# Moving one of the eight batches of compressed cache pages from the last round of the first projection to the second half of the first gate projection

## What is computed

```python
def compress(rows, w):      # rows (B,L,KV,HD), w (CMP_LEN,KV); CMP_LEN 32, CMP_STRIDE 16
    n = L // CMP_STRIDE
    seg = rows[:, :n * CMP_STRIDE].reshape(B, n, CMP_STRIDE, C_KV_HEADS, HEAD_DIM)
    first = jnp.einsum('bnrhd,rh->bnhd', seg, w[:CMP_STRIDE])
    second = jnp.einsum('bnrhd,rh->bnhd', seg, w[CMP_STRIDE:])
    return first[:, :-1] + second[:, 1:]
...
    h = h + mix
    h = h + jax.nn.sigmoid(h @ prm['w_ple_gate'][i]) * (p[i] @ prm['w_ple'][i])
```

## Time and profile before

| | |
|---|---|
| median of 3 runs | 2066.35 us (2063.69 to 2068.67) |
| span of the profiled execution | 2066.1 us |
| PE busy | 1915.6 us, 93% |
| DVE busy | 1063.6 us, 51% |
| ACT busy | 833.9 us, 40% |
| chain that ended last | PE 77%, DVE 11%, SP's queue 4%, DMA 3% |
| line 1541 in that chain | 44% of the span |

### The profile page before, as it was taken

The page is one execution under the profiler, slowest core; times in us unless marked ns, Lnnn a source line. Parts: engine busy times, 40 slices in busy tenths (PEclk is TensorE's granted clock), DMA queues, the critical chain, the costliest instruction groups (busy, mean ns, idle before and its releaser), DMA issues.

```text
span 2066.1 us, 43255 instructions
## 1 busy us (share of the span) xinstructions
PE 1915.6 (93%) x16603; PEld 1621.0 (78%) x16603; DVE 1063.6 (51%) x1777; ACT 833.9 (40%) x1761; POOL 1.4 (0%) x8
## 2 busy tenths in 40 slices
PE   4999999999999899998999997899999777879998
PEld 3899999888888799798999995444444467769998
DVE  3358777666443544346689665433333322235454
ACT  2344444554344333445755552333323322234454
POOL 0000000000000000000000000000000000000000
PEclk9999999999999799999999999999999899999999
DMA  5788878633877488576555552244444389885454
GB/s 192 232 269 263 263 257 265 206 113 123 267 263 247 146 280 272 203 233 202 157 151 162 162 155 75 92 139 132 136 130 136 116 286 295 286 280 188 170 179 139
DMA packets 306536, 406.05 MB, mean 197 GB/s; under 512 B 18472, under 2 KB 222823, under 8 KB 305088
## 3 DMA queue, kind: packets, MB, share of 16 engines
q1 hardware_dynamic: 306384, 403.94, 61.3%
HBM read 391.43 MB, written 12.45 MB: 195 GB/s over the span
## 4 chain that ended last, share of the span: by engine, by line
PE 77%; DVE 11%; SPq 4%; DMA 3%; issue 2%; ACT 2%; DVEq 0%; ACTq 0%
PE PJ L1541 44%; PE XB L1993 8%; PE XB L1567 4%; PE XB L2004 4%; DVE w_low L980 2%; SPq L490 2%; DVE scr L999 2%; SPq L496 1%; PE XB L1813 1%; PE PJ L1981 1%; PE XB L1656 1%; DMA cring<-in_cache_c_win_kv_dram 1%; PE PJ L1960 1%; PE XB L1585 1%; PE XB L2063 1%
## 5 line engine op out<-in xcount | busy, mean ns | idle before, releaser
L1541 PE MATMUL PJ<-xh,w_up 128*128 128x264 f32 x3072 | 920.2, 300 | 40.1 <-DVE w_low L980 21.5
L1541 PE MATMUL PJ<-xl,w_up 128*128 128x264 f32 x3072 | 881.0, 287 | 0.0
L1541 PE MATMUL PJ<-xh,w_low 128*128 128x264 f32 x3072 | 879.3, 286 | 0.0
L980 DVE TENSOR_TENSOR w_low<-wring,w_up 128x512 fp32r<-128x512 f32 x768 | 524.8, 691 | 606.0 <-ACT w_up L602 595.6
L602 ACT CAST w_up<-wring 128x512 fp32r<-128x512 f32 x768 | 473.3, 619 | 644.7 <-PE PJ L1541 536.9
L1541 PEld LDWEIGHTS PJ<-xh,w_up 128*128 128x128 f32 x3072 | 587.6, 191 | 79.8 <-issue 56.4
L1541 PEld LDWEIGHTS PJ<-xl,w_up 128*128 128x128 f32 x3072 | 587.7, 191 | 1.4
L1541 PEld LDWEIGHTS PJ<-xh,w_low 128*128 128x128 f32 x3072 | 585.6, 191 | 0.0
L1993 PE MATMUL XB<-wring,proj 128*32 128x512 f32 x320 | 167.1, 605 | 1.1 <-DVE proj L1419 0.9
L2004 PEld LDWEIGHTS XB<-const,cring 128*128 128x128 f32 x640 | 70.8, 141 | 86.1 <-ACT wring L926 41.9
L1412 DVE COPY wring<-XB 128x512 f32<-128x512 f32 x80 | 55.3, 691 | 159.6 <-PE XB L2004 159.6
(11 more groups left out here) (301 smaller groups left out, 1448.7 us busy)
## 6 DMA issues: line engine op xcount, KB each, us to landing
wring<-in_w_in_ab_dram SPq DMA_DIRECT2D x144, 512.0 KB, 4.6
cring<-in_cache_c_cmp_kv_dram SPq DMA_DIRECT2D x128, 512.0 KB, 3.9
cring<-in_cache_c_sel_kv_dram SPq DMA_DIRECT2D x256, 256.0 KB, 2.9
wring<-in_w_in_c_dram SPq DMA_DIRECT2D x112, 512.0 KB, 3.7
wring<-in_w_ple_gate_dram SPq DMA_DIRECT2D x64, 512.0 KB, 3.6
cring<-in_cache_a_kv_dram SPq DMA_DIRECT2D x48, 512.0 KB, 5.0
wring<-in_w_out_ab_dram SPq DMA_DIRECT2D x32, 512.0 KB, 5.2
cring<-in_cache_c_win_kv_dram SPq DMA_DIRECT2D x64, 256.0 KB, 4.1
```

The source lines that it names most:

```text
L980: nc.vector.tensor_tensor(w_low[:, e % NE], raw(e), w_up[:, e % NE].bitcast(F32), ALU.subtract).then_inc(sem("w_lo"), 1)
L1541: ins = nc.tensor.matmul(PJ[(2 * bl + c) % 4][:, 0:T], w[:, e % NE, k, tileT(c)], x[:, kx, :], start=(kx == 0 and w is w_up and x is xh), ...
```

## The change

Batch 4 no longer goes with AB1's fifth round. AB1's first four rounds take batches 0 to 3, OUT0 takes 4 and 5 (before 5 and 6), and GATE0 takes 6 in its first four blocks (before 7) and 7 in its last four, which had no pages. The counts of `c_used`, `c_in` and `cmp_free` follow. DVE copies batch 6 out before block 4's splits instead of before block 5's, and batch 7 after the whole gate. SP's loop of AB1 runs four times and the fifth round's quarters are written out.

```diff
-        CMP_A, AK, AV, CMP_B = 0, 80, 104, 128
+        CMP_A, AK, AV, CMP_B = 0, 64, 88, 112
@@ SP
             for m in range(8):
                 for q in range(4):
                     quarter(GATE0 + m, w_g, 0, m, q)
-                    if m < 4:
-                        page(2, 5, m, q)
+                    page(2 + m // 4, 4, m % 4, q)
...
-            sp.wait_ge(sem("c_used"), NP + CMP_B + 48)
+            sp.wait_ge(sem("c_used"), NP + CMP_B + 64)
             sp.dma_start(wg, w_c[:, :, 40 * P:40 * P + 48]).then_inc(sem("wg_in"), 16)
@@ DVE
-                if n % 4 == 3:
+                if n % 4 == 3 and n < 16:
                     compressed(n // 4, n // 4, CMP_A)
...
                 for m in range(8):
-                    if layer == 0 and m == 5:
-                        compressed(2, 7, CMP_B)
+                    if layer == 0 and m == 4:
+                        compressed(2, 6, CMP_B)
...
+                if layer == 0:
+                    compressed(3, 7, CMP_B)
@@ PE
-            ab1_round(4, True)
+            ab1_round(4, True, False)
...
             def beside_gate(m, s):
-                if m < 4:
-                    beside_out(8 + m, s)
+                beside_out(8 + m, s)
```

## The result

| | before | after |
|---|---|---|
| median | 2066.05 us (4 runs, 2063.69 to 2068.67) | 2085.19 us (4 runs, 2082.50 to 2087.97) |
| ratio | | 1.0091, 95% interval 1.0073 to 1.0109 |
| span of the profiled execution | 2066.1 us | 2080.2 us (its time: 2082.59) |

The changed kernel is slower by 19.1 us, 0.9%. The forecast was +3.6 us, and its range ended at +6.7. The two profiled spans differ by less, 14.1 us: after's profiled execution was one of its quicker ones, and before's probably its slowest.

What follows compares the result with a forecast made beforehand. PE was taken to bound the kernel at both places, its chain lying on PE for 77% of the span. Terms of -13.15 + 14.28 + 2.5 = +3.6 us on a 2066.35 median gave 2070 us, range 2066.5 to 2073.0.

Steps and rivals of the forecast that it cites:

- Term 1: AB1's last round without its 16 pages: 12.8 us a block, paced by DVE's split, 51.2 for 64.35 us, -13.15 us.
- rival at PE's pace: AB1's last round: DVE's splits just make it, blocks take 12.53 us; sum +2.5 us, 2068.8; chance 0.13.
- Term 2: Gate blocks 4 to 7 with the pages added: PE-bound, no hidden room, +14.28 us.
- rival of cheaper pages: Gate blocks 4 to 7: pages cost some 6.2 us and not 14.28; 2061.9 in all; chance 0.05.
- Term 3: End of the gate: PE's embedding transposes wait for DVE's two copies of batch 7, nothing hides it, +2.5 us.
- SP's new wait and the spill: SP's queue behind the last page: `wg` issued later, spill landing near 982.5 against 988.0; cost nothing, cover 5 us.
- cold start: CQ's first matmuls at half clock for longer, or a late spill: +6.9 us, 2073.3; chance 0.17.
- SP loses 16 pages from its queue: AB1's last round: DMA engines 0.79 busy and PE not waiting for them, so SP's shorter queue is worth nothing.
- The last section of the prediction: Signs expected in the profile of after; forecast wrong if AB2, OUT0 or layer 1 change length.

Runs made afterwards that it cites:

- e12: Changed kernel with SP's value loop written out, four reciprocals of the norm in AB1's last round left out; 2068.24 us in one run.
- e4: Changed kernel without the join: embedding transposed into banks the pages don't use, so PE doesn't wait for DVE's copies; 2078.49 us, ratio 1.0065.
- e2: Changed kernel with SP's code shifted by 32 more unused semaphore increments, 144 in all by the trace's count; 2071.79 us, ratio 1.0035.
- e1: Kernel before with SP's code shifted by 96 unused semaphore increments, no work moved; 2073.56 us, ratio 1.0037.
- e3: Kernel before with SP's code shifted by 128 unused semaphore increments; 2066.06 us, ratio 1.0002.
- e5: Kernel before with SP's code shifted by 32 unused semaphore increments; 2065.33 us, ratio 0.9994.
- e6: Kernel before with SP's code shifted by 64 unused semaphore increments; 2064.73 us, ratio 0.9994.
- e9: Kernel before with SP's value loop written out as straight code; 2064.15 us, ratio 0.9985.
- e13: Kernel before with SP's code shifted by 224 unused semaphore increments; 2071.39 us in one run.
- e15: Kernel before with SP's code shifted by 112 unused semaphore increments; 2074.75 us in one run.
- e8: Changed kernel with SP's value loop written out as straight code, unshifted; 2067.65 us, ratio 1.0011.
- e7: Changed kernel with SP's code shifted by 32 more and the embedding's transposes freed of the wait for DVE's copies; 2069.98 us, ratio 1.0014.
- e10: Changed kernel with SP's value loop written out and the embedding's transposes freed of the wait for DVE's copies; 2066.76 us, ratio 0.9993.
- e11: Changed kernel with batch 7 neither loaded nor multiplied, its place filled from batch 6's sums, leaving only AB1's lighter round; 2055.71 us, ratio 0.9947.

## Why the prediction was wrong

**Term 1, the round at 51.2 us: right.** 51.31 us, blocks at 12.84, DVE's split ahead of slot 7 as said, and e12 shows the bound itself. The rival at PE's pace is out.

**Term 2, the pages in the gate: right.** Blocks of 15.78, 16.21 and 16.22 us against 15.8, 16.2 and 16.2. The rival of cheaper pages is out.

**Term 3, the join: right in kind, 0.9 us too dear.** 2.5 us were forecast, at least 2.0, and 1.6 measured (e4 against after); PE stands idle for 1.45 us, not 2.3. The step missed is that the last page itself now stands ahead of PE's last sum. DVE's last operation on `hs` starts 1.29 us behind the last matmul of the projection in both kernels (970.57 - 969.28, and 971.67 - 970.38), but PE comes to its last sum 0.82 us behind that matmul in place of 0.12, so 0.7 us of DVE's copies lie beside the page. That the path up to CQ's steady pace came out at +3.56 against +3.6 is luck: 1.4 us more between the spatial mix and the embedding's product made up for it, of which the forecast had nothing.

**SP's new wait and the spill: right.** `wg` was issued 9.5 us later, and ACT lost nothing by it. The spill landed 10.5 us after its issue in place of 7.4, at 984.2, 4.9 us ahead of ACT's first split. The cold start cost nothing that shows: from the transposes to CQ's steady pace it took 17.78 us, and 17.73 before.

**The step that failed** is the one that gave SP's part nothing, in two sentences: "SP loses 16 pages from its queue ...; nothing" and "I would be wrong if AB2, OUT0 or layer 1 change their length, since nothing there is touched". Each instruction that SP gained was priced by its own time in the queue, hidden. None was priced by its place in the code. The change adds 112 instructions to an engine whose loop lies behind them; in the bad stretch that costs two gaps of some 8 us at a point where ACT and PE live from SP's transfers, and 13.4 us of time by the medians (after against e2; 11.6 by the ratios). The last section of the prediction did name the symptom, layer 1 changing its length, but without a mechanism or a chance. It needed one: the rows on the packets and SP's timeline at the jump were in the trace of before. They couldn't have told where the bad stretch lies; they could have made it a rival on the slower side. The Trainium skill's page "Runtime: NRT & Kernel Launch", section "Instruction fetch mechanics", says that a taken branch whose target isn't in the window of code at hand forces a DMA fetch before execution goes on. The trace agrees in kind: 5.84 us of "issue" at the jump, and 15 packets for 6. The page's blocks are of 16 KiB; here the packets of this queue have 8 KB, and the shifts fit a period of 8 KB.

**A second, smaller miss is the profile's place among the runs.** The prediction took the span, 2066.1, for the profiled execution's time. In each later run the time is 2 us or so over the span (2082.59 against 2080.2), so the profiled execution of before took about 2068 and was probably the slowest of its three runs, 2068.67, not 0.25 us under the median. Five other traces with before's layer 0 (e1, e3, e5, e6, e9) reach the embedding's transposes at 965.4 to 968.0, mean 967.0 (e13 to e15 give 966.5), not at 969.85; after, e2 and e8 at 972.8 on the mean. So the cost of the change up to there is +5.8 us, not +3.5. By parts, mean of those three minus mean of those five:

| stretch, by first starts | difference |
|---|---|
| to the transposes behind AB1 (L1610) | -13.3 |
| from there to the spatial mix (L1750) | +0.4 |
| from the mix to the embedding's product (L1817) | +1.8 |
| from there to the gate's first sum (L1524), all of it in the product | +1.0 |
| from the gate's first sum to its last | +14.3 (forecast 14.3) |
| from the last sum to the embedding's transposes (L1837) | +1.6 (forecast 2.5) |

The +1.0 comes from the clock and not from the change: the product takes 17.0 and 17.1 us at a mean granted clock of 0.83 and 0.82 in before and after, and 15.5 us at 0.91 in e5 and e8. Most of the +1.8 sits in the mix, whose matmuls are the same in number. Busy by stretch from its first to just past its last start, before and after; the granted clock is the third number from the end:

```profile
685.63:706.29 20.66, 20.66 (x77) 15.15 (x75) 4.14 (x9) 1.40 (x3) 0.00 (x0) 0.64 0.29 96
```

```profile
671.73:693.61 21.88, 21.88 (x76) 15.96 (x74) 4.13 (x9) 1.40 (x3) 0.00 (x0) 0.59 0.27 88
```

PE is busy throughout in both, and the clock falls to 1.2 GHz within them; after, it falls sooner relative to the work (mean 0.59 for 0.64). By the rows of L1750 the mix takes 19.7 to 20.1 us in the nine traces with before's layer 0, 21.2 to 21.4 in after, e2, e4, e7, e8 and e10, but 19.4 in e11, which has done the same work up to there, and 16.9 in e12. What shifts the fall stays open, and so whether the change brings it; it isn't the gate's pages, which come later. Together: -13.3 + 2.2 + 1.0 + 14.3 + 1.6 = +5.8 us, where e2 measured +5.7 on the medians and +7.2 by its ratio. With e8 the cost is 5.4 us against e9 (0.26%). The three parts that the forecast had come to -13.3 + 14.3 + 1.6 = +2.6 us; the other 3.2 lie mostly where the clock was lower. So without SP's stall the forecast would have been short by 2 to 4 us, inside its range by the medians and just outside by e2's ratio.

## What to carry to other kernels

Where a change adds or removes instructions on an engine that runs a loop further on, ask where that loop will lie, and look at the gap between the last transfer of a pass and the first of the next: a loss in a stage that wasn't touched, with more instruction packets on the page, is this. Test it by a shift of the code or by writing the loop out, before a schedule is judged by its time; here the stall cost more (11.6 to 13.4 us) than the schedule itself (5.7 to 7.2). And place the profiled execution among the runs by its own time, not by its span, before a sum of 3 us is set against it.

## What the runs showed of the hardware

- A jump back on SP stalls or doesn't by the loop's place in packets of 128 instructions. For this loop of 292 instructions, shifts of 0, 32, 64, 80, 128 and 144 are free, and 96, 112 and 224 stall: by the count above, in three packets it is free and in four it stalls.
- A stall is long because the fetch seems to stand behind data: in after the engines moved 341 GB/s until 1696, and only then a packet came and SP went on; in e1 it was 339 GB/s until 1691, with the packet at 1691.3. No run varied the load.
- Two gaps of 6.4 to 8.4 us cost 7.6 us in all in one kernel (e1), 9.2 in a single run of a second (e15) and 11.6 to 13.4 us in a third (after against e2). Their sums are 12.9, 15.3 and 16.4 us, which goes the same way but doesn't explain the whole difference.
- Straight code that starts at the bad place doesn't stall (e8), and written out the loop took 3.1 us less even against a loop in a good place (e9, ratio 0.9985, 0.9974 to 0.9996).
- The same matmuls of the spatial mix took 16.9 to 21.4 us in different kernels, by how soon the granted clock fell from 2.4 to 1.2 GHz.
